# One decoder step on one core: half-size products for a second pair of FFN products, and weight sums made by adding DMAs

## The reference

```python
h = x + mix @ w_out
hn = rms_norm(h, norm_ffn_g)
return h + (jax.nn.silu(hn @ w_gate) * (hn @ w_up)) @ w_down
```

## Time and profile before

| | us |
|---|---|
| time, median of 3 runs | 1216.79 (1215.94 to 1216.95) |
| the profiled execution's own time | 1217.06 |
| its span in the trace | 1215.3 |
| PE busy | 1197.9 (99% of the span) |
| DVE, ACT, POOL busy | 679.3, 438.1, 509.6 |

### The profile page before, as it was taken

How to read it: one execution, slowest core, us unless ns; L and a number is a source line. 1 busy time by engine, 2 the same in 40 slices (tenths; PEclk the granted TensorE clock), 3 DMA queues, 4 the chain that set the end, 5 groups by cost and what they waited for, 6 DMA issues and landing times.

```text
span 1215.3 us, 22908 instructions
## 1 busy us (share of the span) xinstructions
PE 1197.9 (99%) x9257; PEld 1136.5 (94%) x9257; DVE 679.3 (56%) x1133; ACT 438.1 (36%) x828; POOL 509.6 (42%) x420
## 2 busy tenths in 40 slices
PE   7999999999999999999999999999999999999998
PEld 6998779889877799999999999999999999999998
DVE  6888214414677623479555444454554178756665
ACT  7111120000378711355443343334333443445452
POOL 3436023233144341052788768776878640000020
PEclk9999999999999999999999999999999999999999
DMA  5478676343223151012614342245444995323223
GB/s 214 156 281 262 230 262 235 139 174 103 84 92 111 48 185 65 1 45 69 241 48 170 116 149 96 106 175 218 166 173 163 345 342 203 94 88 96 86 74 108
DMA packets 70393, 182.66 MB, mean 150 GB/s; under 512 B 7376, under 2 KB 24464, under 8 KB 66320
## 3 DMA queue, kind: packets, MB, share of 16 engines
q1 hardware_dynamic: 70144, 180.92, 42.5%
q10 hardware_dynamic: 144, 0.27, 0.1%
HBM read 136.33 MB, written 44.83 MB: 149 GB/s over the span
## 4 chain that ended last, share of the span: by engine, by line
PE 48%; DVE 2%; POOL 1%; issue 1%; DMA 0%; ACT 0%; DVEq 0%; ACTq 0%
PE ps L1577 9%; PE ps L1579 9%; PE ps L1578 9%; PE ps L1626 6%; PE ps L1627 6%; PE ps L1628 6%; PE ps L1601 1%; PE ps L1600 1%; PE ps L1602 1%; POOL w_lo L966 1%; DVE norms L2735 1%; DMA w_stage<-in_w 0%; DVE combo_b L2262 0%; POOL w_stage L1009 0%; DVE w_lo L2663 0%
## 5 line engine op out<-in xcount | busy, mean ns | idle before, releaser
L1118 PE MATMUL ps<-act_hi,w_hi 128*128 128x352 f32 x480 | 157.4, 328 | 8.2 <-DVE act_lo L2267 8.2
L1577 PE MATMUL ps<-combo,w_hi 128*128 128x264 f32 x544 | 154.9, 285 | 1.7 <-DVE evac L2651 1.2
L1120 PE MATMUL ps<-act_hi,w_lo 128*128 128x352 f32 x480 | 154.8, 323 | 0.0
L1119 PE MATMUL ps<-act_lo,w_hi 128*128 128x352 f32 x480 | 154.7, 322 | 0.0
L1579 PE MATMUL ps<-combo,w_lo 128*128 128x264 f32 x544 | 154.5, 284 | 0.0
L1578 PE MATMUL ps<-combo,w_hi 128*128 128x264 f32 x544 | 154.3, 284 | 0.0
L1626 PE MATMUL ps<-hid,w_hi 128*128 128x264 f32 x536 | 152.7, 285 | 0.0
L1627 PE MATMUL ps<-hid,w_hi 128*128 128x264 f32 x536 | 152.4, 284 | 0.0
L1628 PE MATMUL ps<-hid,w_lo 128*128 128x264 f32 x536 | 152.3, 284 | 0.0
L966 POOL TENSOR_TENSOR w_lo<-w_stage,w_hi 128x512 fp32r<-128x512 f32 (+1 forms) x51 | 76.2, 1495 | 106.1 <-ACT w_hi L1704 106.0
L1577 PEld LDWEIGHTS ps<-combo,w_hi 128*128 128x128 f32 x544 | 102.2, 188 | 2.1 <-issue 1.4
(11 more groups left out here) (470 smaller groups left out, 3237.1 us busy)
## 6 DMA issues: line engine op xcount, KB each, us to landing
w_stage<-in_w SPq DMA_DIRECT2D x56, 512.0 KB, 4.1
resid<-in_state_k SPq DMA_DIRECT2D x8, 1792.0 KB, 11.0
norms<-in_w SPq DMA_DIRECT2D x22, 512.0 KB, 4.4
t_d<-norms SPq DMA_DIRECT2D x11, 1024.0 KB, 4.9
h_d<-evac SPq DMA_DIRECT2D x36, 264.0 KB, 2.3
v_buf<-in_state_v SPq DMA_DIRECT2D x9, 1024.0 KB, 7.0
resid<-in_xT SPq DMA_DIRECT2D x16, 528.0 KB, 7.3
late<-h_d SPq DMA_DIRECT2D x6, 1056.0 KB, 12.9
```

The lines of the kernel that those rows point to most:

```text
L1118: pe.matmul(out, hi, rhs_hi, start=first, stop=False)
L1119: pe.matmul(out, hi, rhs_lo, start=False, stop=False)
L1120: return pe.matmul(out, lo, rhs_hi, start=False, stop=last)
L1577: pe.matmul(out, hi[:, wk], x_hi[:, k, tk], start=(k == 0 and first), stop=False, skip_group_check=not first)
```

## The change

Pairs now begin at slice 6 (seven pairs); slices 4 and 5 run as single slices. In a pair, the two P4 products of both slices are done as half-size products too (jobs B1 to B4, on another set of token block sums). A pair is thus 10 whole products, A and B: 10 x 24 + 84 = 324 matmuls. B adds its parts by DVE to the kept second gate half; a new step `third_up` adds P7 there first. The token block sums for B are a second group, so `block_step` and `block_high` run twice as often, spread over slices 3 to 5. The weight quarter sums of a pair are made twice (once for A, once for B), all on DVE and in single steps; POOL's fourth sums move to DVE.

The down weight sums no longer pass through the core: SP copies quarters of `w_down` from memory to `t_d` (2.88 MB a copy, four copies), and POOL issues 20 DMAs that add another quarter onto them in memory, during attention, the output projection and the pairs.

SP's order changes with it:

```diff
@@ SP, in the attention phase
             load_second(0)
             load_pair_values(0)
+            sp.dma_start(sums_blocks("P5"), down_blocks(0, 0)).then_inc(sums_copied, 16)
...
             unit(28)
+            sp.dma_start(sums_blocks("P7"), down_blocks(0, 1)).then_inc(sums_copied, 16)
+            sp.wait_ge(sums_added, 16 * 4)
+            for product in ("P6", "P4"):
+                sp.dma_start(sums_blocks(product), sums_blocks("P5")).then_inc(sums_copied, 16)
...
             for k in range(KT):
                 sp.dma_start(res[:, k, :], xT[:, k, :]).then_inc(x_in[k], 16)
```

```diff
@@ POOL
+            def add_block(product, x, y, part):
+                ks = slice(3 * part, min(3 * part + 3, HK))
+                pool.dma_start(sums_blocks(product)[:, ks, :], down_blocks(x, y)[:, ks, :], accum_op=ALU.add
+                               ).then_inc(sums_added, 16)
...
                 spread_reciprocals(b + 4)
+                if g == 0:
+                    pool.wait_ge(sums_copied, 16)
+                add_block("P5", 0, 1, g)
                 spread_reciprocals(b + 5)
...
             for a in PAIRS:
-                fourth_sum_of(a)
...
+                    if (x, product) == (0, "P7"):
...
+                        if 0 <= part < 4:
+                            add_block("P7", 1, 1, part)
+                        elif part >= 4:
+                            add_block("P6", 1, 1, part - 4)
+                    elif (x, product) == (1, "P5"):
+                        if 0 <= part < 4:
+                            add_block("P4", 1, 0, part)
```

```diff
@@ the products of a pair, in PE's order
 PAIR_ORDER = [(0, "P1"), (1, "P1"), (0, "A1"), (0, "P6"), (0, "A2"), (1, "P6"), (0, "A3"), (0, "P7"), (0, "A4"), (0, "P5"),
-              (0, "P4"), (0, "P3"), (1, "P7"), (1, "P5"), (1, "P4"), (1, "P3")]
+              (0, "B1"), (1, "P7"), (0, "B2"), (1, "P5"), (0, "B3"), (0, "P3"), (0, "B4"), (1, "P3")]
```

```diff
@@ ACT, slices 3 and 4
-            keep_p1(3)
-            weight_high(3, "P3")
-            silu_first(3)
...
+            for f in (3, 4):
+                keep_p1(f)
+                weight_high(f, "P3")
+                silu_first(f)
+                weight_high(f + 1, "P1")
+                keep_u2(f)
+                weight_high(f + 1, "P2")
+                block_high(0, 2 * f - 6)
+                keep_p7(f)
+                weight_high(f + 1, "P6")
+                block_high(0, 2 * f - 5)
+                weight_high(f + 1, "P7")
+                silu_second(f)
+                weight_high(f + 1, "P5")
+                weight_high(f + 1, "P4")
@@ DVE, slices 2 to 4
             first_gate(3)
-            block_step(0)
-            block_step(1)
+            block_step(0, 0)
             second_up(3)
...
             second_gate(3)
             first_hidden(3)
...
+            block_step(0, 1)
+            first_gate(4)
+            block_step(0, 2)
```

More of the change, by code:

```diff
@@ L685, in load_raw @@
                         split_ready(sp, key)
+                    if was == "gate" and g in PAIRS:
+                        sp.wait_ge(pair_sum, pair_sums(g, "second", 3))
                 sp.dma_start(raws[at], w[FFN0 + LOAD[what, f]]).then_inc(raw_in[at], 16)
@@ L826, in _ @@
                 load_down(s)
+            for k in range(KT - 2, KT):
+                sp.dma_start(res[:, k, :], res_d[:, k, :]).then_inc(x_in[k], 16)
             store_hidden(0, FT - 1)
@@ L1032, in _ @@
             pool.wait_ge(pv_done, STEPS // 2)
[L1033 to L1034 removed]
+            straight(OUT0 + 3)
+            straight(OUT0 + 4)
+            straight(OUT0 + 5)
+            pool.wait_ge(sums_copied, 64)
+            add_block("P4", 1, 1, 0)
+            straight(OUT0 + 6)
+            add_block("P4", 1, 1, 1)
+            straight(OUT0 + 7)
+            add_block("P4", 1, 1, 2)
+            add_block("P4", 1, 1, 3)
             weight_low(0, "G")
@@ L2720, in pair_second_sums, with first_pair_sum, second_pair_sum @@
+            def first_pair_sum(a, name):
+                w11, w12 = (raw("gate", a + x)[:, 512:768] for x in range(2))
+                if name == "first":
+                    raw_ready(dve, "gate", a)
+                    raw_ready(dve, "gate", a + 1)
+                    if a > PAIR_FIRST:
+                        split_ready(dve, (a - 2, "B3"))
+                else:
+                    split_ready(dve, (a, "A3"))
+                    dve.wait_ge(pair_sum, pair_sums(a + 1, "fourth", 0))
                 dve.tensor_tensor(pair_t[0], w12, w11, ALU.subtract).then_inc(pair_sum, 1)
+            def second_pair_sum(a, name):
+                w12, w22 = (raw("gate", a + 1)[:, 512 + 256 * k:768 + 256 * k] for k in range(2))
@@ new lines, in _ @@
+                third_up(b)
+                put_sub(a, "B", "p6")
+                put_sub(a, "B", "p7")
+                second_up(b)
+                if more:
+                    pair_first_sum(n)
+                put_sub(a, "B", "p5")
+                put_sub(a, "B", "p4")
+                if more:
+                    pair_second_sum(n)
+                first_hidden(a)
+                if more:
+                    first_pair_sum(n, "first")
+                    second_pair_sum(n, "first")
@@ L2990, in _ @@
+                put_sub(a, "B", "p3")
+                if more:
+                    third_pair_sum(n, "first")
+                first_hidden(b)
+                if more:
+                    fourth_pair_sum(n, "first")
+                    pair_first_sum(n + 1)
+                    pair_second_sum(n + 1)
             for f in range(PAIR_END, FT):
@@ L3151, in lay_out @@
     for what in ORDER:
-        if what[1][0] != "A":
+        if what[1][0] not in "AB":
             no += 1
```

423 lines of the change are left out of this document (217 added, 206 removed).

## The result

The changed kernel takes 1226.76 us (median of 4 runs, 1225.25 to 1227.83); the kernel before, beside it on the same chip, 1216.37 (4 runs). The ratio is 1.0085, with a 95% interval of 1.0067 to 1.0102: 10 us slower, where I had forecast 5 us faster. The profiled execution took 1227.83 us.

The account below looks back on a forecast made before the run. Bound taken as PE's matmuls by their pitch, plus seam waits. Terms -4.4 - 2.5 + 0.8 + 0.7 + 0.3 + 0 = -5.1 us from 1217.06 give 1212.0, from the median 1211.7; forecast 1211.8, range 1209.9 to 1213.5, 8 in 10 up to 1223.

Parts of the forecast that it names:

- term 5: Output projection: input tiles queued behind three copies land at 439.5 us, just in time at 336 GB/s; 0 us.
- term 4: Inside a pair: the tightest chains keep about 2 us of slack, so 0 us, and +0.3 for anything overlooked.
- signs of being wrong: Forecast wrong if the wait near 441 us is above 3 us or the pair period above 39.8 us.
- Term 1: Pairs and slices 4 and 5: 36 fewer matmuls on PE at 0.1215 us each, -4.4 us.
- Term 2: FFN entry and first pair: -2.5 us for three old waits, +0.8 back for what stays.
- Term 3: Slice 4: a new PE wait near 618 us for ACT's keep of P1, +0.7 us, up to +2.
- rival (b): Pairs: chains break through adding DMA issue or stretched DVE sums, 3.5 to 10 us in seven pairs; chance 0.12.
- rival (a): Output projection waits once for its first input tile near 441 us, copies below 290 GB/s; 1226.5 at 208; chance 0.32.
- my 336: Copy rate of 336 GB/s assumed ahead of the input tiles, taken from the down phase.
- my own sign: Output projection: PE's wait near 441 us, with DVE waiting for the input tile, gives the copy rate by its length.

Follow-up runs that it names:

- adds_moved: On top of x_first, both adding DMAs of a pair moved to later places in POOL's order, same bytes: 1210.83 us, ratio 0.9950.
- second_add_moved: On top of x_first, only the second adding DMA of a pair moved, behind the issue of the next pair's weight loads: 1212.56 us, ratio 0.9968.
- tiny_adds: On top of x_first, the pairs' twelve adding DMAs issued at the same places with 1/32 of the bytes: 1212.23 us, ratio 0.9962.
- x_first: Changed kernel with the last two copies, and POOL's four additions onto P4, put behind the input and output projection weight tiles: 1217.93 us, ratio 1.0009.
- no_gate: Changed kernel with the second and third copies waiting for nothing and reading a quarter of the down weights: 1224.64 us, ratio 1.0067.
- both_moved: As adds_moved, with the odd slice's fourth sum also put behind the additions of p5 and p4: 1210.97 us, ratio 0.9953.
- first_add_moved: On top of x_first, only the first adding DMA of a pair moved, behind the low of the odd slice's P7: 1221.25 us, ratio 1.0034.

## Why the prediction was wrong

Two terms failed: term 5, put at 0 and measured at 10.1 us, and term 4, put at 0.3 and measured at 7.1. Both of my signs of being wrong came: the wait near 441 us is 7.4 us (above 3), and the pair period 40.7 (above 39.8). Most of both failures is one mistake. I priced an adding DMA by its issue, and not by the 8.3 to 12.5 us until it lands and by what its bytes do to the transfers beside it.

**Term 1, the matmuls: right.** 36 fewer, and a pair is 39.40 us where nothing else interferes (adds_moved).

**Term 2, the old seams: right.** The waits of 1.2, 0.8 and 0.5 us went; 0.4 us on POOL stays at the entry, where I had 0.8. The 1.4 us on POOL at the first pair is not theirs: it belongs to the addition's issue (gone in adds_moved, there in second_add_moved, 1.1 in tiny_adds).

**Term 3, slice 4: right in kind, smaller.** PE waits 0.4 us for ACT's keep, at 618.8 us in x_first and near 628 in the changed kernel, where everything is later by then; I had 0.7.

**Term 4, inside a pair: the step that failed is the pricing of the adding DMAs.** I priced their issue, 1.4 us (measured 1.25, at most 1.46), and found the slack: the loads of the next pair land near 32.5 us, about 2 us early. But I gave the transfer no price. The second addition is issued just ahead of those loads and its bytes move beside them, so that they land in 6.2 us and not 3.5: 2.7 us, more than the slack. POOL starts the next pair late, runs back to back, and DVE's sum beside it is stretched. That is 5.4 us, and 1.4 to 1.7 at the first pair: 7.1 in place of 0.3. I had rival (b) at 3.5 to 10 us with a chance of 0.12; its mechanism had POOL's issue and DVE's sums in it, of which only the second was seen, and as a consequence.

**Term 5, the input tiles: wrong by 10.1 us; the step that failed is what the adding DMA does to the copies.** The wait is the one of rival (a), at the place I named (L1356, near 441 us), but the rival's condition did not come: with nothing beside them the copies moved 316 to 357 GB/s, not below 290, and my 336 lies in that. By my own sign a wait of 7.4 us would have meant 250 GB/s, so the sign misleads. What I had wrong is in four parts. The second copy waits for the last P5 addition, which lands 12.5 us after its issue: 3.2 us. Beside that addition the copies lose, by the estimate above, 4.8 us and not 2: 2.8 us. A lateness of 2.5 us more stays open, against the 1.2 us that my sum had to spare. And a stop of 7.4 us lowers the granted clock: 2.7 us more, for which I had no term. That rival (a) at 208 GB/s gave 1226.5, 0.3 from the measured time, is chance: it has neither that rate nor the 7.1 us in the pairs.

**The sum.** With the measured terms, -4.4 - 2.5 + 0.4 + 0.4 = -6.1 from 1217.06 gives 1211.0; adds_moved, profiled, took 1210.86. Add 7.1 for the additions' places and 10.1 for the copies' place: 1228.2, and the changed kernel took 1227.83. The estimate of 358 GB/s for a copy, worked out from the Trainium skill, HBM Reference, "Specifications (TRN2)", agrees with the first copy while nothing ran beside it (357 GB/s) and is above the later ones (316 and 327); for these the measurement decides. That the page's figure for a pair covers reading and writing together was my reading; the page does not say so.

## What to carry to other kernels

Price a DMA in four ways: what its issue costs the engine, how long it holds the queue for whoever comes behind, when it lands if anything waits for that, and what its bytes do to the loads that are under way, with the slack of those loads beside it. A transfer that nobody waits for belongs behind the issue of the loads that somebody waits for. And when a slow instruction stands in front of a wait (here the fourth sum), test whether it is the cause: removing what delays its engine may be worth more than moving it.

## What the runs showed of the hardware that I had not expected

- An adding DMA from memory to memory of 0.79 MB takes 8.3 us from issue to landing, 95 GB/s. While it is under way a plain 0.5 MB load lands in 6.2 us in place of 3.5, and beside copies the queues move 148 to 218 GB/s in all, where copies alone made 316 to 357. In x_first POOL's second of two such DMAs in a row is issued some 8 us behind the first, and POOL stands meanwhile:

```profile
477.14 1.28 POOL L921 DMA_DIRECT2D t_d<-in_w  x1 [8.57 <-DMA t_d<-t_d]
485.14 1.23 POOL L921 DMA_DIRECT2D t_d<-in_w  x1 [6.72 <-issue]
```

- SP too stands at an issue when megabytes are queued: 8.35 us for 36 KB behind two copies, and in no_gate 17.05 us for the issue of the second and third copy.
- A 512-column sum of DVE can take 0.68 us (adds_moved, at 780.44). The fourth sum took 1.23 us in both_moved, 3.02 in tiny_adds and 4.24 in the changed kernel, and each time it ended 0.55 to 0.57 us after the end of POOL's last low in a row without a gap (750.60, 749.13 and 765.07 us). In these three POOL's row sets its length. Why it slips in between two lows in adds_moved (1.47 us at 745.43) the traces do not say.
- After a stop of 7.4 us PE did 68 matmuls in 10 us at a granted clock of 0.78, and after one of 4.2 us 84 at 0.99 in the same window, with 0.67 in the window of the stop. Stops of 2.1 and 1.9 us have 0.83 in their window (first_add_moved).
